# Hyena tiles with the slab rests on VectorE, the loop unrolled, the head norm in seven parts; the merge as 24 split slabs of which four lie in the last tile

## The reference, cut to what matters

```
# branch A: HGRN2, 8 heads; o is (1, 256, 8, 128)
o   = rmsnorm_2(o, hgrn_norm_g)                       # the head norm: over each head's 128 channels
y_a = (o * silu(og)) @ w_branch_a
# branch B: Hyena, 1024 channels
hy = centred_short_conv(hy, conv_w, conv_b)           # width 3, per channel
x0, x1, v = split(hy, 3)
y_b = x0 * bidirectional_fftconv(v * x1, h_f, h_b, bias)
y_b = y_b @ w_branch_b
# merge
merged = sigmoid(g_a) * y_a + sigmoid(g_b) * y_b
h = h + merged @ w_out
```

## Time and profile before

| what | value |
|---|---|
| median of three runs | 2113.43 us |
| profiled execution, own time | 2114.4 us |
| its span | 2112.6 us |
| TensorE matmul busy | 1991.1 us (94%) |
| VectorE busy | 1308.4 us (62%) |
| ScalarE busy | 969.8 us (46%) |
| GpSimd busy | 395.4 us (19%) |
| chain that ended last | PE 78%, issue 10%, DVE 5%, POOL 5%, ACT 2% |

### The profile page before, as it was taken

How to read it: one execution, slowest core, us unless ns; L and a number is a source line. 1 busy time by engine, 2 the same in 40 slices (tenths; PEclk the granted TensorE clock), 3 DMA queues, 4 the chain that set the end, 5 groups by cost and what they waited for, 6 DMA issues and landing times.

```text
span 2112.6 us, 34107 instructions
## 1 busy us (share of the span) xinstructions
PE 1991.1 (94%) x12134; PEld 1749.1 (83%) x12134; DVE 1308.4 (62%) x2625; ACT 969.8 (46%) x1570; POOL 395.4 (19%) x174
## 2 busy tenths in 40 slices
PE   7998999999899969998888989989999999999998
PEld 6776787778688859998777879989999998888887
DVE  5356556657545557897665239952666756666666
ACT  4436546555544446665331035645444444333333
POOL 0000000000000000001551037886666600000000
PEclk9899999999899989999999999999999999999999
DMA  5242455433355525443331434534444445555554
GB/s 221 69 148 91 160 199 174 155 130 110 105 165 189 188 94 166 149 138 104 101 107 60 150 130 160 176 132 149 141 140 141 140 160 179 194 193 192 195 190 158
DMA packets 85143, 313.89 MB, mean 149 GB/s; under 512 B 9456, under 2 KB 9456, under 8 KB 84592
## 3 DMA queue, kind: packets, MB, share of 16 engines
q1 hardware_dynamic: 85040, 312.49, 44.2%
HBM read 311.40 MB, written 1.05 MB: 148 GB/s over the span
## 4 chain that ended last, share of the span: by engine, by line
PE 78%; issue 10%; DVE 5%; POOL 5%; ACT 2%; DMA 0%; DVEq 0%; POOLq 0%; ACTq 0%
PE ps L395 22%; PE ps L277 21%; PE ps L382 14%; PE ps L1641 5%; POOL wsplit L261 5%; PE ps L2301 3%; PE ps L653 2%; PE ps L1707 1%; PE ps L703 1%; PE ps L1947 1%; PE ps L1950 1%; PE ps L714 1%; PE ps L1161 1%; PE ps L1655 1%; PE ps L580 1%
## 5 line engine op out<-in xcount | busy, mean ns | idle before, releaser
L255 ACT ACTIVATE wsplit<-ring 128x1024 fp32r<-128x1024 f32 x548 | 578.9, 1057 | 503.6 <-PE ps L395 278.1
L261 DVE TENSOR_TENSOR wsplit<-ring,wsplit 128x1024 fp32r<-128x1024 f32 x394 | 481.6, 1224 | 331.1 <-ACT wsplit L255 330.2
L277 PE MATMUL ps<-hsplit,wsplit 128*128 128x256 f32 x5064 | 658.7, 290 | 14.8 <-POOL wsplit L261 11.5
L277 PEld LDWEIGHTS ps<-hsplit,wsplit 128*128 128x128 f32 x5064 | 633.6, 197 | 22.2 <-POOL wsplit L261 12.9
L395 PE MATMUL ps<-wsplit,gsplit 128*128 128x512 f32 x2064 | 472.8, 390 | 2.8 <-DVE gsplit L522 2.8
L395 PEld LDWEIGHTS ps<-wsplit,gsplit 128*128 128x128 f32 x2064 | 386.7, 188 | 87.6 <-issue 4.2
L261 POOL TENSOR_TENSOR wsplit<-ring,wsplit 128x1024 fp32r<-128x1024 f32 x154 | 386.9, 2518 | 319.8 <-ACT wsplit L255 319.6
L382 PE MATMUL ps<-wsplit,hsplit 128*128 128x512 f32 x1248 | 304.2, 401 | 11.9 <-DVE wsplit L261 11.1
L382 PEld LDWEIGHTS ps<-wsplit,hsplit 128*128 128x128 f32 x1248 | 238.9, 193 | 65.0 <-DVE wsplit L261 11.9
L2033 POOL COPY work<-work 128x256 f32 (+1 forms) x8 | 4.6, 570 | 981.3 <-DVE work L2045 981.3
L1641 PE MATMUL ps<-hsplit,wsplit 128*128 128x256 f32 x936 | 128.3, 288 | 0.0
(11 more groups left out here) (305 smaller groups left out, 1709.9 us busy)
## 6 DMA issues: line engine op xcount, KB each, us to landing
ring<-in_weights SPq DMA_DIRECT2D x580, 512.0 KB, 3.3
work<-in_tables SPq DMA_DIRECT2D x1, 2123.0 KB, 12.4
xT<-in_x SPq DMA_DIRECT2D x1, 1024.0 KB, 4.8
work<-in_subkeys SPq DMA_DIRECT2D x1, 1024.0 KB, 15.0
work<-in_decay SPq DMA_DIRECT2D x2, 512.0 KB, 3.9
out_x<-work SPq DMA_DIRECT2D x2, 512.0 KB, 2.6
work<-in_w SPq DMA_DIRECT2D x1, 512.0 KB, 5.5
ring<-in_gain_row SPq DMA_DIRECT2D x1, 512.0 KB, 3.7
```

What stands on the lines that cost most here:

```text
L255: act.activation(wsplit[:, n % RING, 0, :], slab(s), ACT.Copy).then_inc(S("split", "lead"), 1)
L261: eng.tensor_tensor(wsplit[:, n % RING, 1, :], slab(s), wsplit[:, n % RING, 0, :], ALU.subtract).then_inc(S("split", RESTS[stream][0]), 1)
L277: mm = pe.matmul(dst, wsplit[:, n, a, c * P:(c + 1) * P], hsplit[:, b, c, :], start=(c == 0 and t == 0), stop=(c == KC - 1 and t == 2))
```

## The change

- The rests of all Hyena fillers move from GpSimd to VectorE. GpSimd has no work left until pq. The tap copies go away: the matmuls read `filt_sum` and `filt_dif` in place.
- The tiles are written out on all engines (`hyena_tile_tensor`, `hyena_tile_scalar`, `hyena_tile_vector`), with constants in place of registers.
- `hy` is cleared before the HGRN stage. Its memory and that of `u` move so that tile 0's staging, short convolution and `u` can be done in the last head.
- Head norm: squares of heads 0 to 6 in the last head on ScalarE, those of head 7 after it. Sums before tile 0 on TensorE, Sqrt in tile 0 after the `uT` copy, then reciprocal and products in seven parts of 293 columns, one per tile, on VectorE. The output of head 7 goes to another PSUM bank.
- Merge: a stream of 24 split slabs, order `w_branch_a`, `w_branch_b`, `w_out`. The first four are the last tile's fillers. Each group of eight needs its operand (`oall`, `yb`, `merged`) split into `hsplit`; this is done in four or five parts as the previous owner's last slab lets go of columns (`FREED`, semaphore "freed").
- The lists of waits and rests are otherwise as before; pq keeps its rests on GpSimd, under a semaphore of its own.

```
-    def out_project(pe, s0, src, dst, sem):
-        for j in range(KC):
-            project(pe, dst[:, j, :], s0 + j, src).then_inc(sem, 1)
...
+            if l == 3 and last:
+                act.wait_ge(S(st, "o_sb"), HH - 1)
+                act.activation(sq[:, 0:HH - 1, :], oall[:, 0:HH - 1, :], ACT.Square).then_inc(S("hnorm", "squares"), 1)
+            if l == 6 and last:
+                hyena_stage_scalar(act, "hyena", 0, 0)
+        if last:
+            hyena_stage_scalar(act, "hyena", 0, 1)
...
             hgrn_prep_vector(v, own, st, h + 1)
+        else:
+            hyena_gates_vector(v, own, "hyena", 0)
         rests_beside(v, st, h, LEVELS - 1)
         keep_vector(v, st, h, LEVELS)
+        if last:
+            hyena_u_vector(v, own, "hyena", 0)
...
+    def filler(i):
+        return ("hgrn", N_HGRN + 4 + i) if i < N_HYENA - 4 else ("merge", i - (N_HYENA - 4))
...
+    def hyena_tile_scalar(act, st, n):
...
+        act.activation(uT[:, :, :].rearrange("p a c -> p (a c)"), ps[:, 2, 0:T], ACT.Copy).then_inc(S(st, "uT_sb"), 1)
+        if n == 0:
+            hgrn_root_scalar(act, "hnorm")
+        lead_scalar(act, *filler(4 * n + 2))
...
+    def hyena_tile_vector(v, own, st, n):
+        more = n + 1 < KC
+        rest_of(v, *filler(4 * n + 2))
+        if n < NORM_PARTS:
+            hgrn_norm_vector(v, own, "hnorm", n)
+        v.wait_ge(S(st, "kspec"), 2 * n + 1)
...
+        rest_of(v, *filler(4 * n + 3))
+        if more:
+            hyena_gates_vector(v, own, st, n + 1)
+            hyena_u_vector(v, own, st, n + 1)
+        else:
+            gated_a_vector(v, own, "merge", 0)
+        rest_of(v, *filler(4 * n + 4))
+        if n == KC - 2:
+            operand_vector(v, "merge", 0, OPERAND_PARTS[0])
+        rest_of(v, *filler(4 * n + 5))
+        v.wait_ge(S(st, "conv"), n + 1)
...
+    OPERAND_PARTS = ((0, 2), (2, 4), (4, 6), (6, 8)), ((0, 2), (2, 4), (4, 6), (6, 8)), ((0, 2), (2, 4), (4, 6), (6, 7), (7, 8))
+    OPERANDS = oall, yb, merged
...
+    def merge_scalar(act, st):
+        for m in range(4, N_MERGE - 2):
+            if m in (KC - 1, 2 * KC - 1):
+                operand_scalar(act, st, (m + 1) // KC)
+            lead_scalar(act, st, m + 2)
...
-        hybrid_gpsimd(pool, "hyena")
         rests_gpsimd(pool, "pq")
```

More of the change, by code:

```diff
@@ L1967, in hyena_tensor @@
     def hyena_tensor(pe, st):
[L1968 to L1972, removed]
         hgrn_norm_tensor(pe, "hnorm")
+        for n in range(KC):
+            hyena_tile_tensor(pe, st, n)
     def hyena_stage_scalar(act, st, n, part):
@@ L2027, in hybrid_gpsimd @@
-    def hybrid_gpsimd(pool, st):
-        pool.wait_ge(S("split", "rest_hybrid"), N_HGRN + 6)
-        pool.wait_ge(S(st, "pads"), 1)
-        def tile(n, turn, u_, more):
-            pool.tensor_copy(taps_now[:, 0, :, :], filt_sum[:, :, bass.ds(n * P, P)])
-            pool.tensor_copy(taps_now[:, 1, :, :], filt_dif[:, :, bass.ds(n * P, P)]).then_inc(S(st, "taps"), 1)
-            for k in range(more):
-                rest_of(pool, "hgrn", N_HGRN + 4 * u_ + 6 + k, turn, 12)
-            pool.wait_ge(S(st, "spectra"), n + 1)
-        with pool.Fori(0, 2) as turn:
-            for u_ in range(3):
-                tile(turn * 3 + u_, turn, u_, 4)
-        tile(6, 2, 0, 2)
-        tile(7, 2, 1, 0)
+            act.activation(gate_b[:, n, :], ps[:, 7, T:2 * T], ACT.Sigmoid).then_inc(S(st, "gate_b"), 1)
@@ new lines, in hyena_vector, with operand_parts, wait_freed @@
+    def hyena_vector(v, own, st):
+        for n in range(KC):
+            hyena_tile_vector(v, own, st, n)
+    OPERAND_PARTS = ((0, 2), (2, 4), (4, 6), (6, 8)), ((0, 2), (2, 4), (4, 6), (6, 8)), ((0, 2), (2, 4), (4, 6), (6, 7), (7, 8))
+    OPERANDS = oall, yb, merged
+    def operand_parts(w):
+        return sum(len(OPERAND_PARTS[x_]) for x_ in range(w))
+    def wait_freed(act, w, part):
+        c1 = OPERAND_PARTS[w][part][1]
+        if c1 < KC:
+            act.wait_ge(S("split", "freed"), len(FREED) * w + FREED.index(c1 - 1) + 1)
+        elif w == 0:
+            act.wait_ge(S("hyena", "in2"), HH)
+        else:
+            act.wait_ge(S("merge", "done"), w * KC)
@@ new lines, in branch, with merge_slab @@
+    def branch(m):
+        j = m % KC
+        if m // KC == 1:
+            return YB[:, j, :] if j < KC - 1 else Y[:, KC - 2, :]
+        return Y[:, j, :]
+    def merge_slab(pe, st, m):
+        n = slab_split(pe, st, m, 0)
+        w = m // KC
+        for c in range(KC):
+            if m % KC == 0:
+                for part, (c0, _) in enumerate(OPERAND_PARTS[w]):
+                    if c0 == c:
+                        pe.wait_ge(S(st, "operand"), operand_parts(w) + part + 1)
+            for t, (a, b) in enumerate(TERMS):
+                mm = pe.matmul(branch(m), wsplit[:, n, a, c * P:(c + 1) * P], hsplit[:, b, c, :],
+                               start=(c == 0 and t == 0), stop=(c == KC - 1 and t == 2))
+                if c == 0 and t == 0:
+                    mm.then_inc(ring_used, 1)
+            if m in (KC - 1, 2 * KC - 1) and c in FREED:
+                mm.then_inc(S("split", "freed"), 1)
+        mm.then_inc(S(st, "done"), 1)
@@ new lines, in merge_tensor, with gated_a_vector @@
+    def merge_tensor(pe, st):
+        for m in range(4, N_MERGE):
+            merge_slab(pe, st, m)
+    def merge_scalar(act, st):
[3 more added lines that the diff above has]
+            lead_scalar(act, st, m + 2)
+    def gated_a_vector(v, own, st, p):
+        v.wait_ge(S(st, "done"), 2 * p + 2)
+        own(v.tensor_tensor(merged[:, 2 * p:2 * p + 2, :], gate_a[:, 2 * p:2 * p + 2, :], Y[:, 2 * p:2 * p + 2, :], ALU.mult))
@@ new lines, in gated_b_vector @@
+    def gated_b_vector(v, own, st, j0, j1):
+        v.wait_ge(S(st, "done"), KC + j1)
+        both = prod_a[:, 0:j1 - j0, :]
+        src = branch(KC + j0) if j1 == j0 + 1 else YB[:, j0:j1, :]
+        if j1 == j0 + 1:
+            own(v.tensor_tensor(prod_a[:, 0, :], gate_b[:, j0, :], src, ALU.mult))
+        else:
+            own(v.tensor_tensor(both, gate_b[:, j0:j1, :], src, ALU.mult))
+        v.tensor_tensor(merged[:, j0:j1, :], merged[:, j0:j1, :], both, ALU.add).then_inc(S(st, "merged"), j1 - j0)
+        v.wait_ge(S(st, "merged"), j1)
@@ L2556, in _ @@
         hyena_scalar(act, "hyena")
+        merge_scalar(act, "merge")
         norm_scalar(act, "n5", xT, S("merge", "x"), 2, 2, leads="pq")
```

296 lines of the change are left out of this document (153 added, 143 removed).

## The result

The changed kernel takes 2062.14 us (median of four runs, 2057.94 to 2066.56), the kernel before 2113.27 (median with a fourth run, 2106.12 to 2114.21). The ratio is 0.9765, 95% interval 0.9735 to 0.9796: 43 to 56 us less. Forecast were 2068, with 2061 to 2080 as range, and 45.8 us of gain. The profiled execution took 2057.94 us, with a span of 2056.2.

A forecast was written before the change was run, and what follows sets the result against it. TensorE was taken to idle in the tiles, waiting for VectorE, which GpSimd's rests held up. Savings 19.8 + 0.3 + 24.2 + 1.5 = 45.8 us gave 2068 us, range 2062 to 2076, or 2061 to 2080 with the first rival.

The forecast's parts named there:

- Tiles: All eight tiles at 17.38 us plus 1.1 of wait, 140.1 us where 159.9 were: 19.8 saved.
- The tight place: VectorE's rest for the next tile's first filler, 0.7 us in hand; tile 0's chain late, 1.1 us of wait.
- The rival that the waits stay without GpSimd: Tiles: VectorE's own chain makes TensorE wait, tiles keep 20.53 us, time 2090; chance 0.05.
- The rival that VectorE is the bound: Tiles: VectorE's load sets the pace, a tile takes 19 us, time 2079; chance 0.1.
- Before tile 0: Up to tile 0's first turn: costs against idle time worked through, turn at 986.3 instead of 986.55, 0.3 us saved.
- The clearing: Clearing `hy`, 0.70 us, now before the HGRN stage; a third hidden by ScalarE's table load, cost 0.5.
- Merge: Twenty slabs at 2.95 us plus 1.7 of waits, 60.7 us where 84.95 were: 24.2 saved.
- the change to `yb`: Merge's second operand: lead and rest of slab 9 come behind its split, 0.4 us of wait.
- the change to `merged`: Merge's third operand: last gate product, split and slab 17's rest behind the last matmul, 1.3 us of wait.
- Behind it: After the merge: 1.0 us of waits at pq and 0.5 for a square go, 1.5 us saved.
- Table switches: ScalarE, tile 0 and n5: 1.28 us per load, no drain; rival of doubled cost adds 2.6, time 2071, chance 0.06.
- The series rival: Merge fed one slab at a time, 6.0 us each, twenty slabs 120 us, time 2129; chance 0.02.

The follow-up runs named there:

- pieces: Changed kernel with VectorE's six long two-operand instructions in the selection of the experts cut in four each: 2055.09 us, ratio to before 0.9727.
- the control run: The changed kernel run again with nothing altered, beside two further variants: 2063.47 us, ratio to before 0.9757.

## Why the prediction was right

Point by point, by its own steps. The mechanism and the pace of the tiles held; two small terms, 0.3 us before tile 0 and 0.5 behind the merge, did not.

- **Tiles: 140.1 us forecast, 139.45 measured.** The pace taken from the one undisturbed tile, 17.38 us, held (17.32). VectorE carries four rests and the norm without setting the pace. The tight place was where the text put it: tile 0's late lead makes TensorE wait for the first rest of tile 1, 1.08 us against 1.1. What I missed was how much of the room comes from the split of the convolution: on the kernel before, with the rests on VectorE but the convolution whole, a tile takes 18.63.
- **The cause of the old waits** is shown, not argued: GpSimd's rests put 1.49 us back before the turn of `yspec`, idle GpSimd work that reads does the same, and work that only writes does nothing. The rival that the waits stay without GpSimd has fallen. The rival that VectorE is the bound has fallen for this order of work, but lies close: with the unsplit convolution, 18.63 us a tile, TensorE waits for a rest in six of them, 6.4 us together.
- **Before tile 0: 0.3 us saved forecast; this did not come out.** The clearing costs the 0.5 booked (11.64 us of idle time before the stage's first matmul, 11.14 before). From that matmul to the first turn are 196.22 us before and 196.02 to 196.09 in seven profiles with the new order: together 0.3 us lost, not saved. The 1.35 us more in the first 48 matmuls, which no term had, are in these. In the two profiles where they are fast (194.69 and 194.71) 1.0 is saved.
- **Merge: 60.7 us forecast, 59.43 measured; here the slab's pace was mis-sized.** In one unbroken run matmuls start 0.12 us apart, so a split slab takes 2.88 us (seven slabs in the 20.41 us above, less the tail), not the 2.95 of a filler between other matmuls: 1.4 us on twenty. What is left, 59.43 - 57.6 = 1.8 us, are starts more than 0.12 us apart. They lie where the text put them: about 0.3 at slab 9, behind the change to `yb` (0.4 booked), 1.4 behind the change to `merged` (1.3 booked), among them the two waits of 0.36 and 0.31, and 0.2 at the first matmul. No run undoes the split of the merge slabs alone, or the move of the norm's sums: that split slabs are faster than plain ones, 2.88 against 3.46 us, is read from the two traces.
- **Behind it: 1.5 us forecast**, 3.4 in the pair. Over the ten profiles without pieces this stretch runs from 876.1 to 881.5 us, so only the vanished waits at pq (1.0 us of the earlier trace rows; now none between 1191 and 1262) are sure. The 0.5 booked for a late square gave nothing: the square starts 0.6 us earlier against the residual, but the Sqrt waits for the sums. From n5's first matmul to the next transposition are 10.47 us before and 10.46 after.
- **Table switches** cost their row and no more: 1.28 us at 980.14 with ScalarE at work until 980.13 and again from 981.43.

```profile
979.74 0.39 ACT L2014 ACTIVATE work<-ps 128x256 f32<-128x256 f32 x1 [2.82 <-PE ps L1970]
980.14 1.28 ACT L1928 ACT_TABLE_LOAD   x1
981.43 1.97 ACT L1928 ACTIVATE work<-ps,eps_tile 128x2048 f32<-128x2048 f32 x1
...
1179.84 1.28 ACT L343 ACT_TABLE_LOAD   x1
1181.85 0.47 ACT L343 ACTIVATE picks<-ps,eps_tile 128x256 f32<-128x256 f32 x1 [0.73 <-PE ps L349]
```

The extra 1.38 us that the Trainium skill gives for a drain (ScalarE: Activation LUTs, "What ACT_TABLE_LOAD costs") isn't there in tile 0, neither before the load nor behind it. At n5 the load begins right behind the square before it, and the 0.73 us behind it are the wait for the sums, too short for a drain of 1.38; the measurement decides.

The forecast of 2068 was 6 us over the median. The stretch T accounts for 1.8 of it (45.8 us measured where 44.0 were booked). By the medians the change gains 51.1 us in the pair and 49.1 in the control run; that the sum of 45.8 agrees with T's 45.8 to the digit is chance, since it also holds 1.8 us for other places. What T and the 1.0 us at pq leave is within what executions differ by. The series rival had nothing: of the twenty slabs one waited for its rest, 0.31 us.

## What to carry to other kernels

Look in the timeline for a short two-operand VectorE instruction that lasts as long as the GpSimd instruction beside it (here 2.36 us beside 2.41, and 0.42 alone); moving GpSimd's reading work to VectorE can be right even where VectorE is the busier engine, if its chain is the one that TensorE waits for. Find one undisturbed turn of the loop and take its pace as the floor, then follow the in-order queue to the instruction with the least reserve. The same hold works the other way: a long VectorE instruction off the critical path can hold a GpSimd instruction on it (here a rest of 2.4 us took 6.45), and cutting it in pieces helps as long as VectorE has idle time to pay with.

## What the runs showed of the hardware that was not expected

- GpSimd with 9.5 us of clearings a tile costs VectorE and TensorE nothing (T 198.87 against 198.88); with 10.4 to 12.0 us of two-operand differences it costs 34.3 us in eight tiles.
- The hold falls on each instruction, not on each column: four products of 1024 columns take 13.35 us between GpSimd's rests, where one of 4096 takes 6.44.
- Some VectorE instructions with one tensor operand are held as well: in the run with rests on GpSimd a TENSOR_SCALAR of 256 columns took 2.38 us beside a rest of 2.38, where 0.41 is its time alone. A TENSOR_REDUCE of 4096 columns doesn't hold a rest: in the control run the rest beside it took 2.38 us.

```profile
1056.01 2.38 POOL L263 TENSOR_TENSOR wsplit<-ring,wsplit 128x1024 fp32r<-128x1024 f32 x1 [2.65 <-ACT wsplit L257]
1056.16 2.38 DVE L2055 TENSOR_SCALAR work<-work 128x256 f32<-128x256 f32 x1
```

```profile
1334.92 4.42 DVE L2343 TENSOR_REDUCE work<-work 128x256 f32<-128x4096 f32 x1
1337.06 2.38 POOL L263 TENSOR_TENSOR wsplit<-ring,wsplit 128x1024 fp32r<-128x1024 f32 x1
```
